# A streaming encoder layer: prompt attention with alternating heads, values in two strips of 64 columns and sums of weights in four of 32

## What is computed

```python
proj = rms_norm(x, ln1) @ w_in                    # q, k, v of 8 heads, forget logits, LRU inputs
q = rms_norm(q, q_gain); k = rms_norm(k, k_gain)
c = jnp.cumsum(log_sigmoid(f + b_f), axis=1)
s = q @ k.T / sqrt(64) + c[:, None] - c[None, :]  # per head
s = where(key <= query, s, -inf)
attn = softmax(s, axis=-1) @ v                    # (1024 x 1024) @ (1024 x 64), causal
```

## Time and profile before

| | |
|---|---|
| median of three executions | 1529.18 us |
| the profiled execution | 1532.99 us, of it the span from first to last instruction 1531.2 us |
| TensorE busy in the span | 1430.0 us (93%) |
| VectorE, ScalarE, GpSimd busy | 735.2, 420.8, 83.1 us |
| mean granted TensorE clock | 0.966 of full |
| first projection of pair 0, 1, 2, 3 | 54.35, 155.90, 249.52, 344.17 us |
| first projection of the LRU | 439.18 us |
| projections of pair 1, 155.90 to 203.72 us | 47.82 us, granted clock 1.00 |

### The profile page before, as it was taken

How to read it: one execution, slowest core, us unless ns; L and a number is a source line. 1 busy time by engine, 2 the same in 40 slices (tenths; PEclk the granted TensorE clock), 3 DMA queues, 4 the chain that set the end, 5 groups by cost and what they waited for, 6 DMA issues and landing times.

```text
span 1531.2 us, 19242 instructions
## 1 busy us (share of the span) xinstructions
PE 1430.0 (93%) x7499; PEld 1238.8 (81%) x7499; DVE 735.2 (48%) x1186; ACT 420.8 (27%) x741; POOL 83.1 (5%) x119
## 2 busy tenths in 40 slices
PE   4969989899898993998999999999999999999997
PEld 3765967859577881887989988999899988999896
DVE  6355364553534646675444354444444444444444
ACT  5124233242334546231312211221112211221110
POOL 2510101101000000000000000000000000000000
PEclk7989999999999996999999999999999999999999
DMA  6023432514222112111111110111011110111004
GB/s 186 7 74 85 127 78 74 145 36 122 63 76 67 30 57 94 58 43 43 55 42 55 42 41 27 55 55 41 17 51 55 41 41 27 55 42 53 14 28 124
DMA packets 133130, 92.87 MB, mean 61 GB/s; under 512 B 22358, under 2 KB 122710, under 8 KB 133076
## 3 DMA queue, kind: packets, MB, share of 16 engines
q1 hardware_dynamic: 133076, 92.14, 21.0%
HBM read 78.24 MB, written 9.68 MB: 57 GB/s over the span
## 4 chain that ended last, share of the span: by engine, by line
PE 87%; DVE 6%; ACT 2%; DMA 2%; issue 1%; SPq 1%; POOL 1%; ACTq 0%; DVEq 0%
PE psum L1469 25%; PE psum L1470 24%; PE psum L1471 24%; PE psum L1691 4%; PE psum L1647 1%; PE psum L1675 1%; DVE tops L1203 1%; PE psum L1678 1%; PE psum L1535 1%; PE psum L1772 1%; POOL rs L690 1%; PE psum L1557 1%; DVE cross_qk L1195 0%; PE psum L1793 0%; PE psum L1582 0%
## 5 line engine op out<-in xcount | busy, mean ns | idle before, releaser
L1437 DVE TENSOR_TENSOR mix<-psum,mix 128x512 f32<-128x512 f32 x288 | 196.4, 690 | 161.9 <-PE psum L1471 161.9
L1469 PE MATMUL psum<-h_hi,wu_hi 128*128 128x384 f32 x768 | 259.6, 338 | 4.2 <-DVE mix L1391 4.2
L1470 PE MATMUL psum<-h_lo,wu_hi 128*128 128x384 f32 x768 | 259.3, 338 | 0.0
L1471 PE MATMUL psum<-h_hi,wu_lo 128*128 128x384 f32 x768 | 259.2, 337 | 0.0
L1469 PE MATMUL psum<-wd_hi,u_hi 128*128 128x512 f32 x576 | 225.0, 391 | 3.6 <-issue 3.6
L1470 PE MATMUL psum<-wd_lo,u_hi 128*128 128x512 f32 x576 | 224.7, 390 | 0.0
L1471 PE MATMUL psum<-wd_hi,u_lo 128*128 128x512 f32 x576 | 224.6, 390 | 0.0
L1469 PEld LDWEIGHTS psum<-h_hi,wu_hi 128*128 128x128 f32 x768 | 145.4, 189 | 4.9 <-issue 4.4
L1470 PEld LDWEIGHTS psum<-h_lo,wu_hi 128*128 128x128 f32 x768 | 145.3, 189 | 0.5
L1471 PEld LDWEIGHTS psum<-h_hi,wu_lo 128*128 128x128 f32 x768 | 145.3, 189 | 0.0
L981 ACT CAST wd_hi<-raw 128x1024 fp32r<-128x1024 f32 x32 | 32.1, 1049 | 401.4 <-PE psum L1471 399.9
(11 more groups left out here) (257 smaller groups left out, 2124.5 us busy)
## 6 DMA issues: line engine op xcount, KB each, us to landing
raw<-in_w_up_dram SPq DMA_DIRECT2D x32, 512.0 KB, 4.4
raw<-in_w_down_dram SPq DMA_DIRECT2D x32, 512.0 KB, 3.3
k_c<-in_cache_k_dram SPq DMA_DIRECT2D x32, 256.0 KB, 2.9
raw<-in_w_in_dram SPq DMA_DIRECT2D x32, 192.0 KB, 3.9
out_dram<-mix SPq DMA_DIRECT2D x9, 512.0 KB
x_in<-in_x_prompt_dram SPq DMA_DIRECT2D x8, 512.0 KB, 4.0
v_c<-in_cache_v_dram SPq DMA_DIRECT2D x16, 256.0 KB, 4.5
kts<-in_cache_v_dram SPq DMA_DIRECT2D x16, 256.0 KB, 4.1
```

The source lines that it names most:

```text
L1437: nc.vector.tensor_tensor(at, psum[:, 4 + 2 * (t % 2) + half, :].rearrange("p (k n) -> p k n", n=P), at, ALU.add).then_inc(y_added, 1)
L1469: nc.tensor.matmul(out, hi(k), r_hi(k), start=first and k == 0, stop=False)
L1470: nc.tensor.matmul(out, hi(k), r_lo(k), start=False, stop=False)
L1471: last = nc.tensor.matmul(out, lo(k), r_hi(k), start=False, stop=end and k == n - 1)
```

## The change

1. **Order of heads.** Steps alternate between the heads: step 2u is head 0 and step 2u+1 head 1 of one key tile. `pt` has six buffers.
2. **Values in two strips.** `values(u)` does both heads: each multiplies 64 columns of v, head 0 into partitions 0 to 63 of a bank and head 1 into 64 to 127. ScalarE then copies a span's output of both heads at once (`outputs`).
3. **Sums in four strips.** `weight_sums` multiplies 32 columns of ones with the weights of four steps (two key tiles, two heads), each into its own 32 partitions of another bank. VectorE copies the sums of a span in one or two instructions; the two partial sums are added after the way through memory.
4. **Bounds amid projections.** `project` is cut in two halves of 12 matmuls; between the halves of tile 6 stand bounds (0,2) and (0,3), of tile 7 (1,1) and (1,2), of tile 8 (0,4). VectorE reads these ahead of `mean` of that tile. `turn_tops(0, 0)` and bound (1,0) stand behind project(6), bound (1,3) and `turn_tops(1, 0)` behind project(7). The high parts of tiles 4 and 5 are made behind project(6).
5. **Later bounds.** Bounds (1,4) to (1,7), which stood in the second span, are now in the first, each behind its neighbour of head 0; both shifts of the second span stand ahead of step 8.
6. **The rest.** `turn_past` 0, 1 and 2 stand in units 8, 9 and 10 and number 3 behind the last one; ScalarE's copies of `kts` stand behind exponentials 19 and 21 (before 18 and 22). The cached values `v_c` are loaded at the end of a pair and no longer amid the next one's projections. The store of v is one DMA for both heads. The memset of v1's ones is gone, two small ones are new.

The core of the diff:

```diff
 def attention_step(s):
-    if s < 8:
-        return s // 4, 0, s % 4
-    return (s - 8) // 8, 1, (s - 8) % 8
+    return (s % 2, 0, s // 2) if s < 8 else (s % 2, 1, (s - 8) // 2)
...
+    BOUND_ORDER = [("b", 0, 0), ("b", 0, 1), ("b", 0, 2), ("b", 0, 3), ("s", 0, 0),
+                   ("b", 1, 0), ("b", 1, 1), ("b", 1, 2), ("b", 1, 3), ("s", 1, 0),
+                   ("b", 0, 4), ("b", 1, 4), ("b", 0, 5), ("b", 1, 5), ("b", 0, 6), ("b", 1, 6), ("b", 0, 7), ("b", 1, 7),
+                   ("s", 0, 1), ("s", 1, 1)]
...
     def bounds_before(hp, t):
-        return 10 * (t // 4) + 5 * hp + t % 4
+        return BOUND_ORDER.index(("b", hp, t))
...
                 for b in range(2, 6):
                     sp.wait_ge(kc_turned, DEC_B * p + b - 1)
                     past_keys(p, b)
+                sp.wait_ge(den_done, 6 * p + 6)
+                past_values(p, 0)
...
                 for s in range(6, STEPS):
                     exp(s)
...
-                    if s in (18, 22):
-                        sample_past(p, (s - 18) // 2)
-                outputs(1, 1)
+                    if s in (19, 21):
+                        sample_past(p, s - 19)
+                outputs(1)
...
                 for t in range(NT):
                     if p >= 1:
                         samples_meanwhile(p - 1, t)
+                    if t == 6:
+                        bound(0, 2)
+                        bound(0, 3)
+                    if t == 7:
+                        bound(1, 1)
+                        bound(1, 2)
+                    if t == 8:
+                        bound(0, 4)
                     mean(t)
                     norm(t)
...
                     if t == 6:
-                        bound(0, 2)
-                        bound(0, 3)
+                        shift(0, 0)
+                        bound(1, 0)
                         if p >= 1:
                             share_out(p - 1)
                     if t == 7:
-                        shift(0, 0)
-                        bound(1, 0)
-                for t in range(1, 4):
-                    bound(1, t)
-                shift(1, 0)
-
-                bound(0, 4)
+                        bound(1, 3)
+                        shift(1, 0)
+
+                bound(1, 4)
+                bound(0, 5)
                 low(4, 0)
-                bound(0, 5)
+                bound(1, 5)
+                bound(0, 6)
                 low(4, 1)
-                bound(0, 6)
+                bound(1, 6)
                 bound(0, 7)
+                bound(1, 7)
+                shift(0, 1)
+                shift(1, 1)
...
+                    for hp in range(2):
+                        r = head_rows(hp)
+                        last = nc.tensor.matmul(psum[r, 4 if qc == 0 else 0, a0 - qc * SPAN:SPAN], v1[:, kt, r],
+                                                pt[:, (s + hp) % 6, 0:a1 - a0], start=kt == 0, stop=kt == 4 * qc + 3)
+                    last.then_inc(pv_done, 1)
+
+                def weight_sums(kt_of):
+
+                    for i in range(4):
+                        s = 2 * kt_of + i
+                        _, qc, kt = attention_step(s)
+                        a0, a1 = step_queries(s)
+                        last = nc.tensor.matmul(psum[32 * i:32 * i + 32, 5 if qc == 0 else 1, a0 - qc * SPAN:SPAN], ones_s[:],
+                                                pt[:, s % 6, 0:a1 - a0], start=kt < 2, stop=kt >= 4 * qc + 2)
+                    last.then_inc(den_done, 1)
...
                 scores(0)
...
+                scores(1)
+                bound(1, 4)
+                meanwhile = {0: [(0, 5), (1, 5)], 1: [(0, 6), (1, 6)], 2: [(0, 7), (1, 7)]}
+                for u in range(STEPS // 2):
+                    if u == 3:
+                        turn_tops(0, 1)
+                        turn_tops(1, 1)
+                    if u < STEPS // 2 - 1:
+                        scores(2 * u + 2)
+                        scores(2 * u + 3)
+                    values(u)
+                    if u % 2 == 1:
+                        weight_sums(u - 1)
+                    for hp, t in meanwhile.get(u, ()):
+                        bound(hp, t)
+                    if u == 2:
                         turn_qk(NT - 1)
...
+                    if u in (8, 9, 10):
+                        turn_past(p, u - 8)
+                turn_past(p, 3)
```

More of the change, by code:

```diff
@@ L82, in streaming_step @@
     over = ExitStack()
+    k_c = sb(over, "k_c", [P, 2, KP, P])
     v_c = sb(over, "v_c", [P, 4, KP, P])
-    k_c = sb(over, "k_c", [P, 2, KP, P])
-    pt = sb(over, "pt", [P, 3, SPAN])
+    over.close()
+    keys_first = sb(over, "keys_first", [P, 2, KP, P])
+    pt = sb(over, "pt", [P, 6, SPAN])
+    o_own = sb(over, "o_own", [P, 2, P])
     over.close()
@@ L163, in streaming_step @@
     tops = sb(pair, "tops", [P, 2, NT - 1])
-    dens = sb(pair, "dens", [P, SPAN])
+    dens = sb(pair, "dens", [P, 2, SPAN])
     top = sb(pair, "top", [P, 2])
@@ L168, in streaming_step @@
     rden = sb(pair, "rden", [P, 2])
-    o_own = sb(pair, "o_own", [P, 2, P])
     pair.close()
@@ L357, in turned_tops_bank @@
     def turned_tops_bank(hp, qc):
-        return 6 + hp if qc == 0 else 6
+        return 6 + hp
     def step_queries(s):
@@ L573, in _ @@
                 sp.wait_ge(k_out[i], 48 * PAIRS)
-            sp.wait_ge(v_out, 48 * PAIRS)
+            sp.wait_ge(v_out, 32 * PAIRS)
             for j in range(KC):
@@ L1609, in pair_pe, with project @@
             def pair_pe(p):
-                def project(t):
+                def project(t, halfway):
                     if t >= 2:
@@ L1613, in project @@
                         pe.wait_ge(v_done, NT * p + t - 1)
-                    split_product(psum[:, 4 + t % 2, 0:PW3], lambda k: h_hi[:, k, tile(t)], lambda k: h_lo[:, k, tile(t)],
-                                  lambda k: wp_hi[:, k, :], lambda k: wp_lo[:, k, :], KC).then_inc(pair_proj, 1)
+                    for part in range(2):
+                        last = split_product(
+                            psum[:, 4 + t % 2, 0:PW3],
+                            lambda k: h_hi[:, 4 * part + k, tile(t)], lambda k: h_lo[:, 4 * part + k, tile(t)],
+                            lambda k: wp_hi[:, 4 * part + k, :], lambda k: wp_lo[:, 4 * part + k, :], 4, part == 0, part == 1)
+                        if part == 0:
+                            halfway(t)
+                    last.then_inc(pair_proj, 1)
                 def turn_qk(t):
```

219 lines of the change are left out of this document (98 added, 121 removed).

## The result

The change makes the kernel slower: 1580.01 us (median of 4 runs, 1579.34 to 1581.6) against 1528.89 (1528.29 to 1530.81), ratio 1.0324, 95% interval 1.0311 to 1.0336 (the two medians divided give 1.0334, inside it). The forecast was 1572, with 1550 to 1592 as its range: the sign, the place and most of the terms hold, three terms (D, F and G) were mis-sized, and their errors partly cancel. The profiled execution has a span of 1578.2 us beside 1531.2, and the mean granted clock over the whole program is the same, 0.966. That doesn't mean that the clock cost nothing. In the pairs it was low for 65 us where it was 34 before. Before, it was also low for 20 us between 18 and 43 us, ahead of the first projection, and this stretch is missing in the changed kernel's profile; the first projection started at 54.35 with it and at 54.62 without it.

What follows compares the result with a forecast made beforehand. The prediction took TensorE, busy 1430 of 1531 us, as the bound, with its waits for VectorE's reads. Terms A to G sum to +43.5, rounded +43; from a median of 1529.18 it forecast 1572 us, range 1550 to 1592.

Steps and rivals of the forecast that it cites:

- D: First span of attention: seven bounds wait for VectorE's reads, 7.9 us per pair; +31.6, net of old waits +10.1.
- F: Values and sums in the attention: strips run beside each other and save 2.0 us per pair, -8; bounds -14 and +20.
- G: Clock: falls at C and at the end of D, two occasions per pair where one was; +6, bounds 0 and +20.
- A: Middle of projection 6, pairs 1 to 3: bound (0,2) waits 2.4 us for the read of bound (0,0); +7.2.
- B: Middle of projection 7, all pairs: bound (1,1) waits 1.3 us for shift (0,0) behind tile 6's scaling; +5.2.
- C: End of projection 7, all pairs: turn_tops(1, 0) waits 3.45 us for the read of (1,3) behind tile 7's scaling; +13.8.
- E: End of a pair: TensorE idles for the last exponentials and late key block 5, 2.3 us per pair; +9.2.
- rival of the late key blocks: v_c loads delay key blocks 6 and 7, so turn_past 6 waits: +6 to +12 with the clock, 1580; chance 10%.
- estimate of about -1: Values and sums: size F would have at the Trainium skill's 2.38x for three column strips, total some 7 higher.
- strips that don't overlap: Values and sums: the saving part does nothing, +20 on F and more slow clock, +63, so 1592; chance 10%.
- reads that hide: Behind projections: reads finish before needed, A, B, C, old waits and clock loss go, so 1488 (faster); chance 4%.

Runs made afterwards that it cites:

- first experiment: Changed kernel with VectorE's order alone altered, reads and a shift moved into its wait for GpSimd's power between mean and scaling: 1554.3 us, ratio 1.0166.
- fifth experiment: Changed kernel with bounds (0,5) to (1,7) of the attention's first span issued one at a time among scores and values: 1578.6 us, ratio 1.0325.
- sixth: Changed kernel with the edits of first, second and fifth experiment, and bound (1,4) ahead of scores 0, read in tile 8's gap: 1534.5 us, ratio 1.0037.
- second experiment: Changed kernel with ScalarE's second copy of kts behind the last exponential and turn_past 0 to 3 one unit earlier: 1570.9 us, ratio 1.0275.
- third experiment: Changed kernel with values and sums at full width again instead of strips, alternating heads and bounds kept: 1571.7 us, ratio 1.0280.
- seventh: The sixth with values and sums at full width, as in the third experiment: 1533.5 us, ratio 1.0030.
- fourth experiment: Kernel before with six VectorE results read between mean and scaling, and TensorE's bound (1,3), turn_tops (1,0) and bounds (0,4) to (0,7) later: 1507.8 us, ratio 0.9862.

## Where the prediction was right and where wrong

- **A, B, C** (7.2 + 5.2 + 13.8): measured 2.31 three times, 1.07, 1.06, 0.88 and 1.07, and 3.25 four times, 6.9 + 4.1 + 13.0. Right in place and count, and in size but for B, which is 1.1 smaller. Pair 0 has no A, as said. The first experiment shows the cause by taking most of it away.
- **D** (+31.6 against the old 21.5): the chain of reads is right, the size not. I had seven waits per pair, 7.9 us together; there are six, 5.85 together. That of values 0 is missing, since TensorE's own work from 225.81 to the values took 3.34, as long as the scaling took, and the six that are there are mostly 0.1 to 0.4 shorter than named. The span up to scores 8 is 20.4 long and not 18.6, because its last 6.5 us ran at the low clock. D net is +2.1 (17.2 + 3.8 + 2.6 - 21.5) and not +10.1. The fifth experiment shows that it isn't the order of bounds alone, and the sixth that 1.9 of the 5.9 per pair hang on when (1, 4) is read; what limits the other 4.1 no run takes away.
- **E** (+9.2): 4.1 for `pt`, 3.9 for `k_c`, and some for `turn_past` 3 itself; the second experiment gives 7.5 back. The rival of the late key blocks is real in a small part: `turn_past` 6, behind the next projection, waits too, 0.3 to 0.7 and 1.9 in all, inside the 3.9, where its price was 6 to 12.
- **F** (-8): the step that failed. I took the narrow strips' overlap from four matmuls whose switches I didn't price. Two strips of 64 took 1.01 where I had 0.93, and every time out of strips and in again costs 0.2. Measured by the rows F is 0; by the third experiment undoing it gives 6.7 us, by the seventh 1.0. The estimate of about -1, from the 2.38x of the Trainium skill ("TensorE: Matmul & The Clock Gate", Part 3), was nearer. But the trace gives another reason for it: four strips of 32 took 0.99 for 512 columns, much as I had reckoned, and what took the saving back is the switches.
- **G** (+6): the mechanism is right, the size too small. In the prediction's own reckoning (length times what the mean clock lacks of 1) the attention lost 4.9 + 5.4 + 5.3 + 3.4 = 19.0 where it was 11.7, the projections of pairs 1 to 3 another 1.8 + 3.6 + 0, and those of pair 0 3.4 from 110.3 to 117.1: +16. But part of that time TensorE stood anyway, as 7.44 busy of 10.30 us show; with half of TensorE's busy time in each low stretch counted as lost, and the stretch around the wait of 9.0 and the start of pair 0 left out, the loss went from 10.8 to 22.1, so G is +11. This is read from one execution of each kernel, and which stretches are low differs from one to the next: the mean clock of the changed kernel's four executions lies between 0.958 and 0.966. I had counted one fall for C and one for D in each pair: D has its four, C three, A one, and three of D's are longer than I had them.
- **The sum.** 34.1 of waits, 11 of clock and 0 for F make 45 of the 49.3 in the pairs. At least a part of the rest sits in the projections: those of pair 3 ran at a clock of 1.00 and are 9.7 longer, 6.6 by the waits A, B and C, 0.5 by that of `turn_past` 6 and 1.4 by the moved bounds. What the other 1.2 are (a projection that is taken up again behind other work, perhaps) no run shows. So of the 6 by which the forecast for the pairs was too low, F (8), G (5) and the rest (4) are on one side, D (8) and small excesses of A, B, C and E (3) on the other.
- **The range.** Two of its rivals were summed wrongly. With strips that don't overlap F is +20 in place of -8, which is 28 more than the forecast and not 20, so this case ends at 1600 and not at 1592. With reads that hide, the 9.2 of E would stay, so that case is 1497 and not 1488. The measured 1580 lies inside either way. That it lies 8 from the forecast is partly luck, since D on one side and F, G and the rest on the other nearly cancel.
- The rival of reads that hide (faster) names the right place, 3.3 us behind a projection. Read in the gap, the kernel before did become faster (fourth experiment). The changed kernel didn't: with all mended it still waits 26.9 us and is at 1534.5 (sixth).

## What to carry to other kernels

When one engine's result has to be read by an engine that runs a chain with another, look for the place inside the chain at which that engine stands idle, and read there; here 1.1 us of gap per tile were worth 24 us in one kernel and 9 in the other, with not one instruction more or less. Issue ahead of a waiting step what has been read already, and put between a product and the step that needs its read more work than the chain is long. A saving in the array's use by strips counts only if few switches go with it: here 0.43 us saved in two units went into leaving and entering strips twice.

## What the runs showed that I had not expected

- The clock's fall can be had back in full: the same attention takes 47.2 us at a mean clock of 0.93, and 41.8 at 1.00, with 11 us less waiting over four pairs. A wait costs more than its length where it brings a low stretch, here 1.6 to 1.7 times: the first experiment returned 23.1 us in the pairs for 14.6 of waits, the fourth 19.0 for 11.0.
- No single wait in D is over 1.32 us, and the clock fell there in every pair. It is several waits close together, in a stretch where TensorE's work between them is short, that it followed.
- With strips the low stretch at the end of the first span lasted 10.2 us in three of four pairs, and 6.8 in all four at full width (third experiment). But in the first experiment, in strips too, it was 6.8 in three of four. Whether strips are the cause, or only when the stretch begins, is open; it is where the 6.7 us of the third experiment would come from.
- Spreading the bounds gave nothing alone, and up to 12 us together with an earlier read of (1, 4) and the reads in the gap.
